# Loading the first tokens ahead of the weights in the input projection of a hybrid encoder

## What is computed

```python
def trunk(x, ln_emb_g, ln_emb_b, w_in, ...):
    x = layer_norm(x, ln_emb_g, ln_emb_b)
    for l in range(DEPTH):
        x = encoder_layer(x, w_in[l], ...)
    return x

def encoder_layer(x, w_in, ...):
    proj = x @ w_in
    ...
```

## Time and profile before

| | |
|---|---|
| median of three runs | 2505.41 us |
| profiled execution, time and span | 2505.09 us, 2503.4 us |
| PE busy | 2407.8 us (96%) |
| DVE busy | 1595.8 us (64%) |
| ACT busy | 1093.8 us (44%) |
| POOL busy | 181.0 us (7%) |
| DMA moved | 547.21 MB, mean 219 GB/s |

### The profile page before, as it was taken

The page is one execution under the profiler, slowest core; times in us unless marked ns, Lnnn a source line. Parts: engine busy times, 40 slices in busy tenths (PEclk is TensorE's granted clock), DMA queues, the critical chain, the costliest instruction groups (busy, mean ns, idle before and its releaser), DMA issues. The chain is left out here.

```text
span 2503.4 us, 35397 instructions
## 1 busy us (share of the span) xinstructions
PE 2407.8 (96%) x12254; PEld 2104.1 (84%) x12254; DVE 1595.8 (64%) x2228; ACT 1093.8 (44%) x1748; POOL 181.0 (7%) x252
## 2 busy tenths in 40 slices
PE   5999988999999979999999999999999999999998
PEld 4888868899788857888899989999888888888886
DVE  7655175766556577666666676666455587669667
ACT  3111133888511134444555555555433344444442
POOL 1000000212122210000000000000000010001001
PEclk9999979999999989999999999999999999999999
DMA  7875545422255765555766686667866669877974
GB/s 253 326 270 215 195 170 160 149 76 71 89 173 214 274 257 204 214 195 209 288 219 244 230 304 222 229 239 270 282 215 193 191 201 331 230 225 238 315 224 137
DMA packets 220011, 547.21 MB, mean 219 GB/s; under 512 B 21568, under 2 KB 90944, under 8 KB 200192
## 3 DMA queue, kind: packets, MB, share of 16 engines
q1 hardware_dynamic: 202592, 481.05, 55.2%
q0 software_dynamic: 17312, 64.76, 8.0%
HBM read 365.37 MB, written 180.36 MB: 218 GB/s over the span
## 5 line engine op out<-in xcount | busy, mean ns | idle before, releaser
L63 PE MATMUL e_bank<-e_hi,e_lo 128*128 128x512 f32 x1120 | 435.8, 389 | 0.4 <-DVE e_lo L1950 0.4
L65 PE MATMUL e_bank<-e_hi 128*128 128x512 f32 x1120 | 435.7, 389 | 0.0
L64 PE MATMUL e_bank<-e_lo,e_hi 128*128 128x512 f32 x1120 | 435.7, 389 | 0.0
L63 PE MATMUL u_bank<-u_x_hi,u_wa_lo 128*128 128x384 f32 (+1 forms) x768 | 272.4, 355 | 5.4 <-DVE u_x_first L1532 2.9
L65 PE MATMUL u_bank<-u_x_hi,u_wa_hi 128*128 128x384 f32 (+1 forms) x768 | 271.4, 353 | 0.0
L1950 DVE TENSOR_TENSOR e_lo<-e_raw,e_hi 128x896 fp32r<-128x896 f32 (+1 forms) x168 | 189.3, 1135 | 119.9 <-ACT e_hi L1921 119.5
L1921 ACT CAST e_hi<-e_raw 128x896 fp32r<-128x896 f32 (+1 forms) x168 | 165.2, 983 | 208.1 <-PE e_bank L65 196.2
L63 PEld LDWEIGHTS e_bank<-e_hi,e_lo 128*128 128x128 f32 x1120 | 210.2, 188 | 44.9 <-DVE e_lo L1950 1.2
L64 PEld LDWEIGHTS e_bank<-e_lo,e_hi 128*128 128x128 f32 x1120 | 210.2, 188 | 43.7
L65 PEld LDWEIGHTS e_bank<-e_hi 128*128 128x128 f32 x1120 | 210.2, 188 | 43.6
L63 PE MATMUL u_bank<-u_x_hi,u_wb_lo 128*128 128x384 f32 (+1 forms) x576 | 205.0, 356 | 9.1 <-DVE u_x_rest L1532 9.1
(11 more groups left out here) (244 smaller groups left out, 4685.8 us busy)
## 6 DMA issues: line engine op xcount, KB each, us to landing
u_w_sum<-s_ws SPq DMA_DIRECT2D x34, 1024.0 KB, 4.8
c_vt_raw<-w_ff SPq DMA_DIRECT2D x24, 1024.0 KB, 7.8
c_q_raw<-w_ff SPq DMA_DIRECT2D x24, 1024.0 KB, 8.1
s_h<-c_k_raw SPq DMA_DIRECT2D x32, 768.0 KB, 7.2
e_raw<-s_t SPq DMA_DIRECT2D x96, 256.0 KB, 3.8
e_raw<-s_h SPq DMA_DIRECT2D x112, 192.0 KB, 2.8
a_w_raw<-w_ff SPq DMA_DIRECT2D x18, 1024.0 KB, 8.3
s_h<-c_k_raw SPq DMA_DIRECT2D x96, 192.0 KB, 2.4
```

Source lines behind the costliest of these rows:

```text
L63: tensor.matmul(out, w_lo, m_hi, start=first, stop=False, skip_group_check=again)
L64: tensor.matmul(out, w_hi, m_lo, start=False, stop=False, skip_group_check=again)
L65: return tensor.matmul(out, w_hi, m_hi, start=False, stop=last, skip_group_check=again)
```

## The change

SP now issues everything of the start, in a new order: token tile 0, `gain`, `shift`, token tiles 1 to 3, the identity, then the eight `w_first` blocks, then the rest blocks. The constants have a semaphore each. DVE takes the moments of a tile and normalises it before it turns to the next. The eight subtractions of `w_first` move from DVE to POOL, laid between the four `inverse_std_of`, with a semaphore of their own, `w_first_split`. On that semaphore SP's rest blocks 2 to 4 now wait, and PE's unit 0. POOL no longer loads the first token tiles; its loads of the next group follow behind its last subtraction.

```diff
         @block.sync
+            for j in range(TPG):
+                sp.dma_start(x_in[:, j, :], x[j * P:(j + 1) * P, :]).then_inc(x_first_ld[j], 16)
+                if j == 0:
+                    sp.dma_start(gain[:], ln_g.partition_broadcast(P)).then_inc(gain_in, 16)
+                    sp.dma_start(shift[:], ln_b.partition_broadcast(P)).then_inc(shift_in, 16)
+            sp.dma_start(ident[:], ident_d).then_inc(ident_in, 16)
             for k in range(KT):
                 sp.dma_start(w_first[k], w_in[k * P:(k + 1) * P, 0:FC]).then_inc(w_first_ld[k], 16)
-                if k == 4:
-                    sp.dma_start(gain[:], ln_g.partition_broadcast(P)).then_inc(const_in, 16)
-                    sp.dma_start(shift[:], ln_b.partition_broadcast(P)).then_inc(const_in, 16)
-                    sp.dma_start(ident[:], ident_d).then_inc(const_in, 16)
             for k in range(KT):
                 if k >= WR:
-                    sp.wait_ge(w_split, KT + k - WR + 1)
+                    sp.wait_ge(w_split, k - WR + 1)
                 elif k >= 2:
-                    sp.wait_ge(w_split, KT)
+                    sp.wait_ge(w_first_split, KT)
                 sp.dma_start(w_rest[k % WR], w_in[k * P:(k + 1) * P, FC:]).then_inc(w_rest_ld[k % WR], 16)
...
         @block.gpsimd
-            load_x(0, True)
...
-            for j in range(TPG):
-                inverse_std_of(j)
+            inverse_std_of(0)
+            inverse_std_of(1)
+            w_low_first(0)
+            inverse_std_of(2)
+            for k in range(1, 4):
+                w_low_first(k)
+            inverse_std_of(3)
+            for k in range(4, KT):
+                w_low_first(k)
...
         @block.vector
             for j in range(TPG):
-                w_low_first(2 * j)
                 moments_of(j)
-                w_low_first(2 * j + 1)
-            dve.drain()
-            dve.wait_ge(const_in, 48)
-            for j in range(TPG):
-                dve.wait_ge(rstd_done, j + 1)
-                normalise(0, j)
+                dve.drain()
+                normalise(0, j, True)
             xt_lows(0)
...
         @block.tensor
-            pe.wait_ge(const_in, 48)
+            pe.wait_ge(ident_in, 16)
...
                         if first and m in (0, FC // P):
-                            pe.wait_ge(w_split, (KT if m else 0) + k + 1)
+                            pe.wait_ge(w_split if m else w_first_split, k + 1)
```

More of the change, by code:

```diff
@@ L129, in embed_project @@
         bank = al.ps("bank", [P, 8, 512])
-        const_in, mhalf_set = al.sem("const_in"), al.sem("mhalf_set")
+        gain_in, shift_in, ident_in, mhalf_set = al.sem("gain_in"), al.sem("shift_in"), al.sem("ident_in"), al.sem("mhalf_set")
         w_first = [w_raw[:, k * FC:(k + 1) * FC] for k in range(KT)]
@@ L137, in embed_project @@
         w_hi_done, w_split = al.sem("w_hi_done"), al.sem("w_split")
+        w_first_split = al.sem("w_first_split")
+        x_first_ld = al.sems("x_first_ld", TPG)
         x_ld, x_free = al.sems("x_ld", TPG), al.sem("x_free")
@@ L225, in body @@
                         load_quad(g, 3)
-            sp.wait_ge(w_split, 2 * KT)
+            sp.wait_ge(w_split, KT)
             with sp.Fori(0, NG - 1) as g:
@@ L239, in _, with load_x @@
         def _(pool):
-            def load_x(g, first):
+            def load_x(g):
                 for j in range(TPG):
-                    if not first:
-                        pool.wait_ge(x_free, (g - 1) * TPG + j + 1)
+                    pool.wait_ge(x_free, (g - 1) * TPG + j + 1)
                     pool.dma_start(x_in[:, j, :], x[bass.ds(g * GRP + j * P, P), :]).then_inc(x_ld[j], 16)
@@ L258, in inverse_std, with w_low_first @@
                 pool.tensor_tensor(rstd[:], var_eps[:], mhalf[:], ALU.pow).then_inc(rstd_done, 1)
-            load_x(0, True)
+            def w_low_first(k):
+                pool.wait_ge(w_hi_done, k + 1)
+                pool.tensor_tensor(w_lo[:, k, 0:FC], w_first[k], w_hi[:, k, 0:FC].bitcast(F32), ALU.subtract
+                                   ).then_inc(w_first_split, 1)
             pool.memset(mhalf[:], -0.5).then_inc(mhalf_set, 1)
@@ L263, in _ @@
             pool.wait_ge(mhalf_set, 2)
-            for j in range(TPG):
-                inverse_std_of(j)
+            inverse_std_of(0)
[7 more added lines that the diff above has]
+                w_low_first(k)
             with pool.Fori(1, NG) as g:
-                load_x(g, False)
+                load_x(g)
                 inverse_std(g)
@@ L271, in _ @@
         def _(dve):
[L272 to L275, removed]
             def w_low_rest(k):
@@ L282, in moments_of @@
             def moments_of(j):
-                dve.wait_ge(x_ld[j], 16)
+                dve.wait_ge(x_first_ld[j], 16)
                 for h in range(2):
@@ L290, in moments @@
                 for j in range(TPG):
-                    dve.wait_ge(x_ld[j], g * 16 + 16)
+                    dve.wait_ge(x_ld[j], g * 16)
                     for h in range(2):
@@ L297, in moments, with normalise @@
                 dve.drain()
-            def normalise(g, j):
+            def normalise(g, j, first=False):
+                if first and j == 0:
+                    dve.wait_ge(gain_in, 16)
                 dve.scalar_tensor_tensor(xg[:, j % 2, :], x_in[:, j, :], mv[:, j, 0:1], gain[:], ALU.subtract,
@@ L302, in normalise @@
                 dve.drain()
+                if first:
+                    dve.wait_ge(rstd_done, j + 1)
+                    if j == 0:
+                        dve.wait_ge(shift_in, 16)
                 dve.wait_ge(turned, g * KT + KT)
```

## The result

| | before | changed |
|---|---|---|
| median (runs) | 2503.65 us (16) | 2510.04 us (16) |
| lowest to highest | 2500.36 to 2508.79 | 2506.32 to 2512.94 |
| profiled span | 2503.4 us | 2509.1 us |

The ratio is 1.0022, with a 95% interval of 1.0015 to 1.003. The change costs 0.2%: a little, but clear of the noise. The medians lie 6.4 us apart. 2510.5 us was forecast, which was +5.4 us on the 2505.09 us of the profiled execution.

The account below looks back on a forecast made before the run. PE sets the time, so its start shifts the total: subtractions end at 29.1, plus 8.2 gives ACT free at 37.3 against 31.91, +5.4 us. 2505.09 + 5.4 = 2510.5 us; range 2503.5 to 2515.

Parts of the forecast that it names:

- The start is the total: PE's first matmul of unit 0: the change of the total equals the change of that start, +5.4 us.
- Token branch: Token loads and DVE's norm: tile 0 lands at 5.1 us; tile 3's `x_nrm` ends at 25.2, against 31.33 before.
- Price of a subtraction: One `w_first` subtraction on POOL: 0.97 us, between 0.39 and 1.35; DVE takes 0.51.
- POOL and DVE: Shared SBUF ports: POOL waits while DVE runs two-operand passes; DVE going first, POOL's last subtraction ends at 29.1 us.
- Stretch to ACT free: From POOL's last subtraction to ACT's cast of rest block 4 ending: 8.2 us, bounds 6.5 and 10.0; 7.1 before.
- Sum: ACT free at 29.1 + 8.2 = 37.3 us against 31.91, so +5.4 us and 2510.5 us in total.
- Cheap POOL: Rival, 15%: a POOL subtraction costs 0.39 us, ACT is free at 32.4 to 33.5, +0.5 to +1.6, 2506 us.
- POOL dear, loads shared: Rival, 22%: costly subtractions and shared loads before ACT's rest block 4 cast; end plus stretch reaches 39.4; +7.8 to +9.6, 2514.
- Token branch decides: Rival, 3%: the tokens set PE's start, 25.7 us in place of 33.36, giving 2497.4 us.

Follow-up runs that it names:

- The third experiment: The changed kernel, but POOL loads the second group's tokens only once rest block 4 is cast; 2506.67 us, ratio 1.0018 to the kernel before.
- the first experiment: The changed kernel, but ACT casts `xt_hi` behind rest block 1 instead of behind rest block 4; 2497.95 us, ratio 0.998 to the kernel before.
- its repeat: The changed kernel with ACT casting `xt_hi` behind rest block 1, run again beside other kernels; 2497.17 us, ratio 0.9974 to the kernel before.

## Why the prediction was right

- *The start is the total.* Right: +5.5 at the first matmul, +5.7 in the span, the gaps in the projection behind it unchanged.
- *Token branch.* Tile 0 landed at 4.18, where 5.1 was taken. Most of that was lost to a wait that was priced at nothing: `shift` landed late, and the first `x_nrm` waited 0.94 us, where tiles 1 and 2 wait about 0.45 for `rstd` alone. That pass ended at 9.50 (9.8 forecast), the last one at 25.07 (25.2).
- *Price of a subtraction.* 0.97 forecast, 0.99 measured (the line of L265 under the result). The Trainium skill's figure (GPSIMD Engine Reference, section Elementwise — side-by-side cycle accounting) led to an estimate of 0.84, 15% low here.
- *POOL and DVE.* That POOL waits for DVE held: an addition of 0.19 took 1.17, a subtraction up to 1.98. The direction that no row had shown exists too: `x_nrm` took 2.01 in place of 1.28 when a subtraction had started 0.06 us ahead of it, as the Trainium skill says (SBUF — State Buffer, section Who interferes with whom), though not for the whole of what was left: DVE lost 0.73 where some 0.93 of POOL's 0.99 us was still to run. I had let DVE go first; with POOL first and DVE held up the prediction gave 28.8 for the last subtraction, against 27.84 measured. Some 0.4 of that last difference is the tiles' being ahead (`rstd` of tile 2 was there at 17.42 and not 17.8), and twice 0.2 is what DVE did not lose; the rest I have not followed. The 29.1 in the sum was 1.3 too late.
- *Stretch to ACT free.* 8.2 was taken, 9.7 measured. This is the second term of the sum that was mis-sized, beside the end of the subtractions: I gave SP's queue a lead over POOL's loads, and the upper bound of 10.0, even sharing, was nearer. The third experiment puts the sharing at 2.8 us of the stretch: without it 6.9, beside 7.1 before.
- *Sum.* The two misses, −1.3 and +1.5, cancel, and ACT was free at 37.52 for 37.3 forecast. That the time came out within 0.5 us of the forecast is partly luck, and twice over: the forecast started from 2505.09 us, 1.4 above the later median of the kernel before, and its +5.4 was 1.0 less than the +6.4 of the medians. The side of zero is not luck: with the end of the subtractions as measured, even the least stretch of 6.5 gives 34.3, still 2.4 behind the 31.91 of before.
- *Cheap POOL* is out by the 0.99. *POOL dear, loads shared* was half true: shared they were, dear POOL was not, and end and stretch added to 37.5, below its 39.4. *Token branch decides* is what ACT's order alone makes of this kernel, 2498 us against the 2497.4 that this rival named: it needed one thing more than the change contained. That the two figures agree so well is chance, since the first matmul came at 27.71 and not at 25.7; DVE's passes were held up by the subtractions, and the kernel before was 2.3 us faster in those runs than the 2505.09 the rival counted from.

## What to carry to other kernels

A load order is as good as the stream that consumes it: before bringing one input forward, follow the work that is pushed back (here the subtractions of the first weights) through every engine whose order is written by hand, and look what stands behind it there. Here a gain of 6 us on one branch became a loss of 6, because three casts of weights that were not yet needed stood ahead of the first tokens' cast, and two loop bounds turned it into a gain of 5 to 6 us. When the first bound is gone, ask which queue was waiting for the same event; here it was SP with its stores, which had next to nothing in hand.

## What the runs showed of the hardware

- DVE and POOL hold each other up when both read two operands from SBUF. DVE lost 0.73 us on a 1.28 us pass in every kernel in which a subtraction started just ahead of it, and nothing where POOL was made to wait. POOL's subtraction took up to 1.98 in place of 0.99 us beside such a pass, and its power 1.44 in place of 0.55.
- Two DMA queues with large loads share the bandwidth: three blocks of 448 KB were taken up 3.2 and 2.4 us apart beside POOL's four loads of 512 KB, and 1.1 and 1.4 us apart without. That is 143 and 191 GB/s for SP's queue, of a mean of 342 over 28 to 36 us, so about half of it.
- PE's granted clock (columns as in the earlier trace rows; the clock stands third from the end). In the changed kernel:

```profile
18.00:22.00 4.00, 1.97 (x8) 1.57 (x8) 3.83 (x5) 1.10 (x2) 4.00 (x4) 0.61 0.00 0
...
26.00:38.00 12.00, 1.10 (x6) 0.70 (x4) 0.00 (x0) 3.30 (x5) 4.12 (x6) 0.50 0.76 289
38.00:43.00 5.00, 4.13 (x10) 3.33 (x11) 4.97 (x9) 3.42 (x7) 0.00 (x0) 0.52 0.00 0
```

In the kernel before, in the first experiment, in its repeat, and with the subtractions left to DVE:

```profile
33.00:37.00 4.00, 4.00 (x11) 2.90 (x10) 4.00 (x8) 2.92 (x6) 0.00 (x0) 1.00 0.13 53
```

```profile
28.00:36.00 8.00, 8.00 (x34) 6.58 (x34) 6.75 (x10) 4.08 (x7) 2.73 (x5) 1.00 0.81 302
```

```profile
26.00:40.00 14.00, 14.00 (x57) 11.37 (x56) 10.06 (x13) 7.10 (x12) 4.65 (x7) 0.84 0.77 297
```

```profile
26.00:40.00 14.00, 3.16 (x8) 2.52 (x9) 5.68 (x11) 6.72 (x11) 0.00 (x0) 1.00 0.53 204
```

The changed kernel starts unit 0 at the lower level (0.52, so mostly 1.2 GHz). The clock had fallen between 18 and 22 us, with PE busy half of that stretch, before the long wait began. The long wait alone does not go with a fall: with the subtractions left to DVE, PE idled 10.9 us in front of unit 0 and the clock stayed at 1.00 (2.4 GHz). One and the same kernel differs as well, 1.00 in the first experiment and partly the lower level in its repeat. What sets the level is not shown here.

What the slower first matmuls cost can be read from their rows. The first nine of unit 0 take 3.94 us in the changed kernel and 3.87 us in the kernel before, where the granted clock reads 1.00; so the clock is no part of the loss. In the first experiment they take 2.67 us and in its repeat 3.51, so on top of the 11.2 us of the start these two executions gained 1.3 and 0.4 us here.
